# Down projections by seven half-size products in two passes, with their weight and activation sums on GpSimd

## The reference, cut to what matters

```python
def hybrid_layer(h, ...):
    proj = h @ w_in                       # 1024 -> attention and state-space channels
    ...
    mix = jnp.concatenate([attn_out, ssd_out], axis=-1) @ w_out
    h = layer_norm(DEEPNORM_ALPHA * h + mix, ln1_g, ln1_b)
    gate, val = jnp.split(h @ w_up, 2, axis=-1)          # 1024 -> 2 x 2816
    gate = depthwise_conv(gate, ffn_conv_w, ffn_conv_b)
    ffn = (jax.nn.silu(gate) * val) @ w_down             # 2816 -> 1024
    return layer_norm(DEEPNORM_ALPHA * h + ffn, ln2_g, ln2_b)
```

## Time and profile before

| | us |
|---|---|
| median of 3 runs (1311.57 to 1311.80) | 1311.78 |
| profiled execution, first to last instruction | 1310.8 |
| TensorE busy | 1301.4 (99%) |
| VectorE busy | 805.6 (61%) |
| ScalarE busy | 581.1 (44%) |
| GpSimd busy | 96.6 (7%) |
| DMA, mean | 99 GB/s |

### The profile page before, as it was taken

One profiled execution on the slowest core, in us unless ns is written; L12 is line 12 of the kernel. 1 busy time (PEld: TensorE's weight loads), 2 busy tenths in 40 slices (PEclk: granted clock), 3 DMA queues, 4 the chain that ended last, 5 costly groups with the idle time before them and its releaser, 6 DMA issues.

```text
span 1310.8 us, 16441 instructions
## 1 busy us (share of the span) xinstructions
PE 1301.4 (99%) x6720; PEld 1074.6 (82%) x6720; DVE 805.6 (61%) x1093; ACT 581.1 (44%) x877; POOL 96.6 (7%) x87
## 2 busy tenths in 40 slices
PE   9999999999999999999999999999999999999997
PEld 8877777889888888888898777788888888888886
DVE  7888778866444444342378987888654444443425
ACT  5765645426333333311276665444453333333112
POOL 2013400001000000000020333000000000000000
PEclk9999999999999999999999999999999999999999
DMA  5422212423333233333143212133233333333332
GB/s 190 161 66 65 60 54 65 177 65 118 96 97 100 97 96 100 130 98 98 54 139 123 65 51 80 49 128 130 81 97 97 97 97 97 97 97 129 97 98 111
DMA packets 33786, 129.17 MB, mean 99 GB/s; under 512 B 3792, under 2 KB 4208, under 8 KB 32560
## 3 DMA queue, kind: packets, MB, share of 16 engines
q1 hardware_dynamic: 33552, 127.84, 30.1%
q0 software_dynamic: 160, 0.29, 0.1%
HBM read 121.82 MB, written 6.29 MB: 98 GB/s over the span
## 4 chain that ended last, share of the span: by engine, by line
PE 97%; DVE 2%; DMA 0%; ACT 0%; issue 0%; DVEq 0%
PE ps L841 18%; PE ps L843 18%; PE ps L842 18%; PE ps L978 9%; PE ps L979 9%; PE ps L980 9%; PE ps L867 4%; PE ps L1194 2%; PE ps L1208 1%; PE ps L1218 1%; PE ps L1228 1%; PE ps L970 1%; PE ps L1163 1%; PE ps L1168 1%; PE ps L1129 1%; PE ps L1178 1%
## 5 line engine op out<-in xcount | busy, mean ns | idle before, releaser
L841 PE MATMUL ps<-hhi,whi 128*128 128x512 f32 x1040 | 407.8, 392 | 0.0
L843 PE MATMUL ps<-hhi,wlo 128*128 128x512 f32 x1040 | 405.1, 390 | 0.0
L842 PE MATMUL ps<-hlo,whi 128*128 128x512 f32 x1040 | 404.8, 389 | 0.0
L1286 DVE TENSOR_TENSOR wlo<-raw,whi 128x1024 fp32r<-128x1024 f32 x208 | 254.2, 1224 | 151.0 <-ACT whi L591 151.0
L591 ACT ACTIVATE whi<-raw 128x1024 fp32r<-128x1024 f32 x208 | 219.3, 1056 | 216.4 <-DMA raw<-in_units 216.4
L841 PEld LDWEIGHTS ps<-hhi,whi 128*128 128x128 f32 x1040 | 195.2, 188 | 41.1 <-issue 1.0
L843 PEld LDWEIGHTS ps<-hhi,wlo 128*128 128x128 f32 x1040 | 195.2, 188 | 41.1
L842 PEld LDWEIGHTS ps<-hlo,whi 128*128 128x128 f32 x1040 | 195.3, 188 | 40.4
L978 PE MATMUL ps<-whi,uhi 128*128 128x512 f32 x352 | 137.1, 390 | 0.0
L980 PE MATMUL ps<-wlo,uhi 128*128 128x512 f32 x352 | 137.0, 389 | 0.0
L979 PE MATMUL ps<-whi,ulo 128*128 128x512 f32 x352 | 136.9, 389 | 0.0
(11 more groups left out here) (185 smaller groups left out, 1488.5 us busy)
## 6 DMA issues: line engine op xcount, KB each, us to landing
raw<-in_units SPq DMA_DIRECT2D x208, 512.0 KB, 3.6
gb<-in_gb SPq DMA_DIRECT2D x5, 1024.0 KB, 5.6
h_kept<-hb SPq DMA_DIRECT2D x2, 2048.0 KB, 9.1
ha<-h_kept SPq DMA_DIRECT2D x2, 2048.0 KB, 8.3
hb<-in_x SPq DMA_DIRECT2D x4, 512.0 KB, 5.8
out_y<-hb SPq DMA_DIRECT2D x8, 256.0 KB, 2.0
cn<-in_cn SPq DMA_DIRECT2D x1, 599.5 KB, 10.1
raw<-in_units SPq DMA_DIRECT2D x2, 128.0 KB, 3.4
```

Of the source, the lines that this page charges most:

```text
L841: mm(out, whi[:, slot, cols], xhi, start=start, stop=False)
L842: mm(out, whi[:, slot, cols], xlo, start=False, stop=False)
L843: return mm(out, wlo[:, slot, cols], xhi, start=False, stop=stop)
L1286: V.tensor_tensor(wlo[:, m % RING, :], raw[:, m % RING, :], f(whi[:, m % RING, :]), ALU.subtract).then_inc(unit_split, 1)
```

## The change

A down projection is a product of 512 tokens x 2816 rows by 2816 x 1024. Its tokens, rows and columns are each halved (A11, A12, A21, A22 and B11, B12, B21, B22; a half of the rows is 11 tiles), and the eight products of halves are replaced by seven, with sums taken ahead of them:

- activations: S1 = A21 + A22, S2 = S1 - A11, S3 = A11 - A21, S4 = A12 - S2 (`activation_sums`: four GpSimd instructions of 128x256 a tile);
- weights, first pass: B12 - B11 and B22 - (B12 - B11) (`first_sums`: two of 128x512 a tile; 768 KB loaded);
- weights, second pass: B21 - B11 and B22 - B12 in one of 128x1024, and a difference of them of 128x512 (`second_sums`; 1 MB loaded, of which B11, B12 and B22 for the second time).

The first pass takes three products (Z = A11 B11, Y, X), the second four (W and the other parts of X, Z, Y). A product is 11 tiles x 2 blocks of 128 tokens x 3 matmuls = 66. Each pass splits its sums: ScalarE copies and VectorE subtracts 128x1536 (weights) and 128x768 (activations) a tile in the first, 128x2048 and 128x1024 in the second. `glu` writes its product unsplit. Between the passes `read_first` adds the first pass's sums from PSUM into the residual `hb`, which now holds ALPHA x h (`scaled_gain`, moved into glu 6 to 13); X, Z and Y go on in the same banks. The last three tiles (layer 1: four) of the second pass are taken block by block. Down weights no longer go through the ring; their places are taken from `raw`, `whi`, `hhi`, `hlo` and the scratch, as those come free.

```diff
-UNITS = U_DOWN + FT
+UNITS = U_DOWN
+STORED = U_DOWN + FT
...
+HALF_K = FT // 2
+TAIL = (3, 4)
...
+        ub = at("ub", 0, [P, HALF_K, 8, SEQ])
+        ubr = at("ubr", 0, [P, HALF_K, 8, SEQ], F32R)
+        a1_place = [(base, 88), (base, 91)] + [(base_hhi, 3 * n) for n in range(5)] + [(base_hlo, 3 * n) for n in range(4)]
+        a1_hi = [at(f"a1_hi{r}", kb, [P, 3, SEQ], F32R, b) for r, (b, kb) in enumerate(a1_place)]
+        e1, e2, q0, q1, q2 = (base, 98), (base, 88), (base_raw, 12), (base_raw, 0), (base_raw, 6)
+        w1_place = [e1, q0, q1, q2, e1, q0, e2, q1, q2, e1, q0]
+        w1_raw = [at(f"w1_raw{r}", kb, [P, 3, 512], F32, b) for r, (b, kb) in enumerate(w1_place)]
+        w1_lo = [at(f"w1_lo{r}", kb, [P, 3, 512], F32R, b) for r, (b, kb) in enumerate(w1_place)]
+        w1_hi = [at(f"w1_hi{r}", (12, 0, 6)[r % 3], [P, 3, 512], F32R, base_whi) for r in range(HALF_K)]
+        w2_place = [(base, 88), (base_hhi, 0), (base_raw, 0), (base_raw, 8), (base, 96), (base, 88), (base_hhi, 0), (base_raw, 8),
+                    (base, 0), (base, 8), (base, 16)]
+        w2_raw = [at(f"w2_raw{r}", kb, [P, 4, 512], F32, b) for r, (b, kb) in enumerate(w2_place)]
+        w2_lo = [at(f"w2_lo{r}", kb, [P, 4, 512], F32R, b) for r, (b, kb) in enumerate(w2_place)]
+        w2_high_place = [(base_hhi, 8), (base_hlo, 0), (base_whi, 0), (base_whi, 8), (base_hlo, 8), (base_hhi, 8), (base_hlo, 0),
+                         (base_whi, 8), (base, 24), (base, 32), (base, 40)]
...
+            def load_first(L, r):
+                if r == 0:
+                    sp_eng.wait_ge(affined, (2 * L + 2) * 2 * NBLK)
+                elif r < 4:
+                    sp_eng.wait_ge(unit_used, unit(L, (None, U_DOWN - 4, U_DOWN - 2, U_DOWN - 1)[r]) + 1)
+                else:
+                    sp_eng.wait_ge(down_used, first_used(L, (0, 1, 1, 2, 3, 4, 5)[r - 4]))
+                sp_eng.dma_start(w1_raw[r][:, 0:2, :].rearrange("p b n -> p (b n)"), down_rows(L, r)).then_inc(w1_loaded[r], 16)
+                sp_eng.dma_start(w1_raw[r][:, 2, :], down_rows(L, HALF_K + r)[:, 512:1024]).then_inc(w1_loaded[r], 16)
+            def load_second(L, r):
+                if r < 5:
+                    sp_eng.wait_ge(down_used, first_used(L, (6, 6, 8, 10, 9)[r]))
+                else:
+                    sp_eng.wait_ge(down_used, second_used(L, (0, 1, 3, 0, 1, 2)[r - 5]))
+                sp_eng.dma_start(w2_raw[r][:, 0:2, :].rearrange("p b n -> p (b n)"), down_rows(L, r)).then_inc(w2_loaded[r], 16)
+                sp_eng.dma_start(w2_raw[r][:, 2:4, :].rearrange("p b n -> p (b n)"), down_rows(L, HALF_K + r)).then_inc(w2_loaded[r], 16)
             for t in range(2):
...
@@ -524,8 +609,40 @@
                     first = idx == 0 and s == 0
                     for j in () if idx == 0 and s else range(4) if first else (2, 3):
                         pool.wait_ge(ln_hi, (idx * NSEQ + s) * 4 + j + 1)
-                        nc.gpsimd.tensor_tensor(pair_of(hlo, s, j), hfm[:, 2 * j:2 * j + 2, :], f(pair_of(hhi, s, j)),
+                        nc.gpsimd.tensor_tensor(pair_of(hlo, s, j), hfms[idx % 2][:, 2 * j:2 * j + 2, :], f(pair_of(hhi, s, j)),
                                                 ALU.subtract).then_inc(entry_low if first else h_lows, 1)
+            linked = [0]
+            def link_pool(ins):
+                linked[0] += 1
+                ins.then_inc(pool_link, 1)
+                pool.wait_ge(pool_link, linked[0])
+            def activation_sums(L, r):
+                a11, s1, s2, a12, s3, s4, a22 = (ub[:, r, n, :] for n in (0, 1, 2, 4, 5, 6, 7))
+                T = nc.gpsimd.tensor_tensor
+                pool.wait_ge(glu_done, L * FT + 2 * r + 2)
+                link_pool(T(s1, s3, a22, ALU.add))
+                link_pool(T(s2, s1, a11, ALU.subtract))
+                T(s4, a12, s2, ALU.subtract).then_inc(act_sums, 1)
+                T(s3, a11, s3, ALU.subtract).then_inc(act_sums, 1)
+            def first_sums(L, r):
+                w = w1_raw[r]
+                pool.wait_ge(w1_loaded[r], L * 32 + 32)
+                link_pool(nc.gpsimd.tensor_tensor(w[:, 1, :], w[:, 1, :], w[:, 0, :], ALU.subtract))
+                nc.gpsimd.tensor_tensor(w[:, 2, :], w[:, 2, :], w[:, 1, :], ALU.subtract).then_inc(w1_sums, 1)
+            def second_sums(L, r):
+                w = w2_raw[r]
+                pool.wait_ge(w2_loaded[r], L * 32 + 32)
+                link_pool(nc.gpsimd.tensor_tensor(w[:, 0:2, :], w[:, 2:4, :], w[:, 0:2, :], ALU.subtract))
+                nc.gpsimd.tensor_tensor(w[:, 0, :], w[:, 0, :], w[:, 1, :], ALU.subtract).then_inc(w2_sums, 1)
             nc.gpsimd.memset(avg[:], 1.0 / D_MODEL).then_inc(avg_set, 1)
...
+                    first_sums(L, r)
+                activation_sums(L, 10)
+                for r in range(4, HALF_K):
+                    first_sums(L, r)
+                for r in range(HALF_K):
+                    second_sums(L, r)
                 if L < DEPTH - 1:
                     lows(2 * L + 2)
...
+            def first_acts(L, r):
+                act.wait_ge(act_sums, (L * HALF_K + r) * 2 + 2)
+                if r >= 2:
+                    act.wait_ge(unit_used, unit(L, U_DOWN - 1) + 1)
+                A(a1_hi[r][:], ub[:, r, 0:3, :], ACT.Copy).then_inc(a1_high, 1)
+            def first_weights(L, r):
+                act.wait_ge(w1_sums, L * HALF_K + r + 1)
+                if r < 3:
+                    act.wait_ge(unit_used, unit(L, (U_DOWN - 4, U_DOWN - 2, U_DOWN - 1)[r]) + 1)
+                else:
+                    act.wait_ge(down_used, first_used(L, r - 3))
+                A(w1_hi[r][:], w1_raw[r][:], ACT.Copy).then_inc(w1_high, 1)
+            def second_acts(L, r):
+                act.wait_ge(act_sums, (L * HALF_K + r) * 2 + 2)
+                act.wait_ge(down_used, first_used(L, r))
+                A(ubr[:, r, 0:4, :], ub[:, r, 4:8, :], ACT.Copy).then_inc(a2_high, 1)
+            def second_weights(L, r):
+                act.wait_ge(w2_sums, L * HALF_K + r + 1)
+                if r < 5:
+                    act.wait_ge(down_used, first_used(L, (6, 9, 10, 9, 10)[r]))
...
+            def product(out, xhi, xlo, w_hi, w_lo, start, stop):
+                mm(out, xhi, w_hi, start=start, stop=False, skip_group_check=True)
+                mm(out, xlo, w_hi, start=False, stop=False, skip_group_check=True)
+                return mm(out, xhi, w_lo, start=False, stop=stop, skip_group_check=True)
...
+                a, w = FIRST[which]
+                rows = slice(v * BLK, (v + 1) * BLK)
+                return product(ps[:, BANKS[which][v], :], a1_hi[r][:, a, rows], ubr[:, r, a, rows], w1_hi[r][:, w, :], w1_lo[r][:, w, :],
+                               r == 0, r == HALF_K - 1)
...
+                a, w = SECOND[which]
+                rows = slice(v * BLK, (v + 1) * BLK)
+                return product(ps[:, BANKS[which][v], :], ubr[:, r, a, rows], ubr[:, r, 4 + a, rows], w2_hi[r][:, w, :], w2_lo[r][:, w, :],
+                               r == 0 and which == "W", r == HALF_K - 1)
+            def first_pass(L):
+                for r in range(2):
+                    pe.wait_ge(a1_split, L * HALF_K + r + 1)
+                    pe.wait_ge(w1_split, L * HALF_K + r + 1)
+                    for which, v, k in (("X", 0, FT - 4), ("X", 1, FT - 3), ("Z", 1, FT - 2), ("Y", 1, FT - 2)):
+                        if r == 0:
+                            pe.wait_ge(glu_done, L * FT + k + 1)
+                        first_product(r, which, v)
+                pe.wait_ge(glu_done, L * FT + FT)
+                for r in range(2):
+                    first_product(r, "Z", 0)
+                    first_product(r, "Y", 0).then_inc(down_used, 1)
+                for r in range(2, HALF_K - 2):
+                    pe.wait_ge(a1_split, L * HALF_K + r + 1)
+                    pe.wait_ge(w1_split, L * HALF_K + r + 1)
+                    for which in "ZXY":
+                        for v in range(2):
+                            done = first_product(r, which, v)
+                    done.then_inc(down_used, 1)
+                for which, full in (("Z", z_full), ("X", x_full), ("Y", y_halfway)):
+                    for r in (HALF_K - 2, HALF_K - 1):
+                        if which == "Z":
+                            pe.wait_ge(a1_split, L * HALF_K + r + 1)
+                            pe.wait_ge(w1_split, L * HALF_K + r + 1)
+                        for v in range(2):
+                            done = first_product(r, which, v)
+                        if which == "Y":
+                            done.then_inc(down_used, 1)
+                        elif r == HALF_K - 1:
+                            done.then_inc(full, 1)
+            def second_ready(L, r):
+                pe.wait_ge(a2_split, L * HALF_K + r + 1)
+                pe.wait_ge(w2_split, L * HALF_K + r + 1)
+            def second_pass(L):
+                idx, tail = 2 * L + 2, range(HALF_K - TAIL[L], HALF_K)
```

(93 more changed lines are left out.)

265 lines of the change are left out of this document (170 added, 95 removed).

## The result

The changed kernel takes 1373.45 us (median of 4 runs, 1372.77 to 1375.61) against 1311.79: ratio 1.0471, 95% interval [1.0456, 1.0486], so 62 us slower. The prediction was 1376 us. The profiled execution's span is 1371.4 us, 60.6 more than before.

A forecast was written before the change was run, and what follows sets the result against it. TensorE bounded the old kernel; in the changed one VectorE and GpSimd, excluding each other, act as one resource. 1310.8 + 60 (both layers) + 4 (clock) = 1374.8 us span, 1376 us with the span's 0.95 us offset; range 1335 to 1402.

The forecast's parts named there:

- 66 matmuls of 0.2267 us a layer go, 29.9 us at most.: Down projections: 462 matmuls a layer in place of 528, 15.0 us a layer less, the most the change can give.
- Alone, each engine fits under TensorE.: Per tile, GpSimd, VectorE and ScalarE each stay below TensorE's 4.08 us (first pass) and 5.44 us (second pass).
- But they don't run side by side.: GpSimd's sums and VectorE's splits exclude each other for the whole instruction; only about 0.14 us of start-up overlaps.
- The rival of no exclusion: Both passes: GpSimd's sums and VectorE's splits overlap freely, 109 and 114 us a layer, 1296 us in all; chance 0.09.
- The rows it was read from: Earlier trace: 298.38 read as GpSimd stretched to 1.42 us by VectorE, 296.20 as a PSUM-operand sum leaving GpSimd undisturbed.
- Per tile: VectorE and GpSimd as one queue: 6.7 us a second-pass tile, 4.8 a first-pass tile, 5.8 with a second-pass split added.
- The other estimate of 2.36: GpSimd's 1024-column sum by the Trainium skill's figure, against 2.40 taken; said to lower the sum by some 3 us.
- Per layer: Pair ends 132.5 us after the up projections, TensorE's 15.0 and 19.7 us follow: 147.4 and 152.2 us, 60 us slower in all.
- The clock: Tail of each down projection may start at half speed after waits: 2 us a layer taken, between nothing and 17.
- The last sums: Before the final norm: they keep their 0.69 us after the last matmul, so the edit costs nothing.
- What TensorE waits for: Waits for splits, not DMA, about 1.3 us a tile; gaps of 5 to 7 us twice ending the first pass, twice before the tail.
- The rival of a low clock: Second pass: the clock stays low throughout, 10.9 us a tile, 84 us more, 1456 us in all; chance 0.04.

The follow-up runs named there:

- e1_narrow: The changed kernel with GpSimd's weight sums cut to one column per 512, semaphores and waits kept: 1284.99 us, ratio 0.9792.
- e4_early: The changed kernel with GpSimd taking the weight sums during the up projections, stored to DRAM and loaded ready in both passes: 1286.23 us, ratio 0.9802.
- e2_memset: The changed kernel with GpSimd's weight sums replaced by memsets of the same place that keep GpSimd as long: 1302.09 us, ratio 0.9923.
- e6_onein: The changed kernel with each pair of GpSimd's weight sums replaced by two in-place multiplications by a constant: 1488.44 us, ratio 1.1341.

## Why the prediction was right

- *66 matmuls of 0.2267 us a layer go, 29.9 us at most.* Right: with the pair out of the way 26.8 us (e1_narrow) and 25.6 us (e4_early) are gained.
- *Alone, each engine fits under TensorE.* Right: e1_narrow, where all but GpSimd's weight sums is left, and e2_memset, where GpSimd is as busy.
- *But they don't run side by side.* Shown by e2_memset against the changed kernel: same GpSimd time, 71 us apart. The rival of no exclusion would have given 1296 us, 109 and 114 a layer; with memsets it is 1302, and 111.6 and 116.2.
- *The rows it was read from.* Two of them say less, or more, than the prediction has them say. The sum of 296.20 overlaps GpSimd's instruction by 0.08 us, less than a handover, so it can't show that a PSUM operand is free of it; e4_early's products from PSUM do. And the VectorE instruction beside 298.38 has one operand, not two, and was itself held up: 1.41 us, where the next of its kind takes 0.81. So exclusion isn't limited to VectorE's two-operand instructions.

```profile
300.00 0.81 DVE L1358 TENSOR_SCALAR hb<-hb,st 128x1024 f32<-128x1024 f32 x1
```

- *Per tile.* Second pass 6.7 forecast, 6.65 measured; first pass 4.8 and about 4.7 (splits at 564.83 and 569.56). Where a second-pass split is added 5.8 was forecast and 7.0 to 8.1 measured (569.56, 576.53, 584.59), as GpSimd, running ahead, puts three sums beside it and not two in two of the three cases; the layer's sum goes by all the work and isn't touched by this. GpSimd's 1024 columns: 2.40 taken, 2.39 the shortest measured. (The other estimate of 2.36 would have taken 0.9 us off the time, 22 x 0.04, and not 3.)
- *Per layer.* Forecast were 149.4 and 154.2 us with the clock's 2 us; up to the last down matmul 146.8 and 151.9 are measured. The last split ends 130.1 us (layer 0) and 129.2 us (layer 1) after the up projections instead of 132.5; the terms as written add to 132.8. For layer 0 most of this is the tile: GpSimd's waits on itself fall into VectorE's turn, some 0.1 us a tile in both passes, and the sum in progress at the start had 0.2 us left, not 1.1. From there TensorE takes 16.7 and 22.7 us instead of 15.0 and 19.7.
- *The clock.* After the last split 7 matmuls of layer 0 and 14 of layer 1 run at or near the lower level, 1.5 and 2.8 us longer: the 2 us a layer hold in sum, and that they do is in part luck, as they were chosen between nothing and 17. I had left out the end of the first pass, where it falls too, at 1 us in layer 0.
- *The last sums.* "Nothing" was wrong by 0.6 us a layer: the changed norm takes the last block in three sums of 128x512 on VectorE where two stood, and the last one starts 0.65 us after TensorE's end (1364.76 for 1364.11; before, 1304.19 for 1304.15).
- *Together.* The pair's work came out 2.4 and 3.3 us shorter, TensorE's time behind it 0.7 us longer in the two layers than the forecast with its 4 us of clock, and the last sums 1.2 us longer: to within the rounding these make the 1371.4 of the span out of 1374.8, and 1373 out of 1376. The mechanism and each large term held; the closeness of the total owes a little to errors of opposite sign.
- *What TensorE waits for.* Splits in both passes, as forecast, and about 1.2 us a tile in the second (6.65 less 5.44) for the forecast's 1.3. Of the two gaps of 5 to 7 us at the end of the first pass one is there (5.04 at 598.44) and one is 3.1; another of 4.9, at 560.26, was not forecast. Before the tail it is 5.6 and 3.8.
- *The rival of a low clock.* It did not come: the granted clock is 1.00 from 607.5 to 657, with waits of 1.2 us a tile. Its price was too high as well: 24 matmuls at 0.427 are 10.2 us a tile, not 10.9.

The Trainium skill (SBUF — State Buffer, Who interferes with whom) says that a GpSimd instruction which only writes SBUF leaves VectorE's two-operand ones alone; e2_memset agrees (2.29 us). The Trainium skill calls the shared ports an exclusive lock in the same section: the sums agree (6.65 us a tile, each waiting for the whole of the other but some 0.13 us), and the one-operand multiplication of e6_onein doesn't, if its splits ran at their own pace once begun.

## What to carry to other kernels

Two engines that are each half idle are not two resources if their instructions exclude each other: add up VectorE's subtractions of two SBUF operands and GpSimd's sums as one queue before moving work between them, and look in the trace for instructions of one form with two durations. What reads PSUM or only writes stayed out of that queue here (e4_early, e2_memset). Work of that pair belongs where TensorE has slack to give, even at the price of a round trip through DRAM: the same seven products are 4.7% slower or 2.0% faster by where their sums are taken. A saving in matmuls is worth only as much as the operands' preparation keeps under it, tile by tile.

## What was not expected of the hardware

GpSimd's multiplication by a constant, one operand in and out in place, took 1.49 us for 512 columns, 4.08 for 1536 and 5.36 for 2048 (the shortest of each, e6_onein), longer than its subtraction of two operands (1.29 for 512, 2.39 for 1024); and VectorE's two-operand instruction seems to have begun before it ended.
